# Block-diagonal recurrence products kept as 64-column halves and multiplied as two 64-row products side by side

## What is computed

```python
def step(state, inp):
    r_t, w_t, k_t, v_t, a_t, b_t = inp
    sa = jnp.einsum('bhvk,bhk->bhv', state, a_t)
    state = (state * w_t[:, :, None, :] + sa[..., None] * b_t[:, :, None, :]
             + v_t[..., None] * k_t[:, :, None, :])
    return state, jnp.einsum('bhvk,bhk->bhv', state, r_t)
state0 = jnp.zeros((B, H, N, N), f32)
_, y = lax.scan(step, state0, inputs)
```

## Time and profile before

| | us |
|---|---|
| Three runs: median (lowest to highest) | 1535.57 (1533.57 to 1537.86) |
| The profiled execution's own time | 1534.63 |
| Its span, first to last instruction | 1532.8 |
| TensorE busy | 1434.3 (94%) |
| VectorE, ScalarE, GpSimd busy | 512.3, 324.5, 64.8 |
| The recurrence, first product to start of `branch` | 1188.93 to 1272.26, 83.3 |

### The profile page before, as it was taken

How to read it: one execution, slowest core, us unless ns; L and a number is a source line. 1 busy time by engine, 2 the same in 40 slices (tenths; PEclk the granted TensorE clock), 3 DMA queues, 4 the chain that set the end, 5 groups by cost and what they waited for, 6 DMA issues and landing times.

```text
span 1532.8 us, 21740 instructions
## 1 busy us (share of the span) xinstructions
PE 1434.3 (94%) x9246; PEld 781.6 (51%) x9246; DVE 512.3 (33%) x881; ACT 324.5 (21%) x476; POOL 64.8 (4%) x32
## 2 busy tenths in 40 slices
PE   8989999999999989989989998978999999999998
PEld 6543333333333333333333333328778885499997
DVE  1753111212111111112112111137797446365665
ACT  0531000101100000001001000025655220244442
POOL 0000000000000000000000000000000000023231
PEclk9999999999999999999999999999999999999999
DMA  9699999999999999999999999984452106145552
GB/s 363 259 379 386 428 427 427 428 429 428 428 428 428 429 428 428 428 429 428 428 428 428 428 429 429 428 360 133 151 165 63 49 2 247 41 164 192 179 190 82
DMA packets 44685, 491.44 MB, mean 321 GB/s; under 512 B 4960, under 2 KB 5472, under 8 KB 13184
## 3 DMA queue, kind: packets, MB, share of 16 engines
q1 hardware_dynamic: 44496, 490.66, 77.9%
q10 hardware_dynamic: 144, 0.13, 0.0%
HBM read 489.73 MB, written 1.05 MB: 320 GB/s over the span
## 4 chain that ended last, share of the span: by engine, by line
PE 63%; DMA 28%; DVE 5%; ACT 3%; issue 1%; POOL 0%; SPq 0%; DVEq 0%; ACTq 0%
DMA ring<-in_w_exp 17%; PE bank L778 14%; PE bank L807 9%; DMA work<-in_w_exp 7%; PE bank L836 6%; PE bank L837 6%; PE bank L838 6%; DMA spare<-in_w_exp 3%; PE bank L736 2%; PE bank L724 2%; PE bank L1176 2%; PE bank L673 2%; PE bank L1214 2%; DMA ring<-in_w_lora 1%; PE bank L594 1%; PE bank L624 1%
## 5 line engine op out<-in xcount | busy, mean ns | idle before, releaser
L778 PE MATMUL bank<-ring,spare 128*64 128x512 f32 x1344 | 302.2, 596 | 25.2 <-DMA ring<-in_w_exp 25.2
L1782 DVE TENSOR_SCALAR work<-bank 128x512 f32<-128x512 f32 x32 | 22.1, 692 | 741.2 <-PE bank L778 741.2
L778 PEld LDWEIGHTS bank<-ring,spare 128*64 128x64 f32 x1344 | 92.9, 136 | 221.0 <-issue 160.0
L807 PE MATMUL bank<-ring,spare 128*64 128x512 f32 x672 | 148.8, 595 | 14.7 <-ACT spare L1340 14.7
L778 PE MATMUL bank<-work,spare 128*64 128x512 f32 x576 | 129.7, 595 | 8.2 <-DMA work<-in_w_exp 8.2
L836 PE MATMUL bank<-work_parts,ring_parts 128*128 128x256 f32 x472 | 131.4, 278 | 4.5 <-DVE work_parts L1841 4.5
L1336 ACT ACTIVATE work<-work 128x512 f32<-128x512 f32 x32 | 20.2, 631 | 536.0 <-DVE work L1782 536.0
L837 PE MATMUL bank<-work_parts,ring_parts 128*128 128x256 f32 x472 | 131.9, 280 | 0.0
L838 PE MATMUL bank<-work_parts,ring_parts 128*128 128x256 f32 x472 | 131.8, 279 | 0.0
L807 PEld LDWEIGHTS bank<-ring,spare 128*64 128x64 f32 x672 | 46.9, 137 | 103.2 <-issue 90.4
L836 PEld LDWEIGHTS bank<-work_parts,ring_parts 128*128 128x128 f32 x472 | 89.7, 190 | 5.6 <-issue 4.9
(11 more groups left out here) (395 smaller groups left out, 1688.0 us busy)
## 6 DMA issues: line engine op xcount, KB each, us to landing
ring<-in_w_exp SPq DMA_DIRECT2D x126, 2048.0 KB, 34.6
work<-in_w_exp SPq DMA_DIRECT2D x54, 2048.0 KB, 34.6
spare<-in_w_exp SPq DMA_DIRECT2D x12, 2048.0 KB, 31.4
ring<-in_ffn_up SPq DMA_DIRECT2D x22, 1024.0 KB, 5.3
ring<-in_ffn_down SPq DMA_DIRECT2D x22, 512.0 KB, 3.5
ring<-in_w_in SPq DMA_DIRECT2D x2, 2048.0 KB, 18.5
ring<-in_w_out SPq DMA_DIRECT2D x4, 1024.0 KB, 17.4
ring<-in_w_k SPq DMA_DIRECT2D x4, 1024.0 KB, 5.2
```

The lines of the kernel that those rows point to most:

```text
L778: ins = pe.matmul(to[n2 * CAP:(n2 + 1) * CAP, :], x_e[:, 2 * j + kk, :], w[:, b, kk, n2 * BANK:(n2 + 1) * BANK], start=False, stop=j == UP ...
L807: ins = pe.matmul(y_bank[n2 * CAP:(n2 + 1) * CAP, :], hidT[:, k % 4, k // 4 * CAP:(k // 4 + 1) * CAP], w[:, kk, n2 * BANK:(n2 + 1) * BANK] ...
```

## The change

- The masked matrices keep, for each row of 128 tokens, only the 64 columns of that row's own half. Their tiles (Mb, MA, MoT, NK, P2, PU) shrink from 128 to 64 columns a head, and so do the six masks. "X2" gets a tile of its own.
- Each 128x128 product becomes two 64x64 products, `rows = pair_rows(c2)` for c2 = 0, 1: operands and output lie in partitions 0 to 63 for the one and 64 to 127 for the other, in the same PSUM bank.
- `products` uses two banks instead of four and `key_products` the other two. `key_products` no longer waits for "Mb".
- `products(0, 0)` comes before the wait for pT2_ready; `key_products(0, 0)` and `products(0, 1)` come before the attention product. The second tile row's `products` go into the first one's chunk loop, after chunks 1 and 2 (batch 1 first). All `outputs` come before the chunk loop.
- The wait for x0 moves from "p8" to "x1". VectorE's U2 becomes two instructions a batch instead of four, and its rT two instead of one.

The core of the diff:

```diff
+            PAIRS = range(TT)
+            pair_rows = lambda c2: slice(c2 * HD, (c2 + 1) * HD)
 def products(tt, b):
-                        pe.matmul(B[2 * half][:, i2 * P:(i2 + 1) * P], ar[k, i, 0, cols], b_hat[k, i, cols],
+                            pe.matmul(B[2 + half][rows, i2 * HD:(i2 + 1) * HD], ar[k, i, 0, cols], b_hat[k, i, cols],
 def key_products(tt, b):
-                pe.wait_ge(rec_ready, count(vector_steps, "Mb", tt, b))
...
-            pe.wait_ge(pT2_ready, 1)
             pe.wait_ge(gate_ready, 6)
             products(0, 0)
-
+            pe.wait_ge(pT2_ready, 1)
+            key_products(0, 0)
             pe.wait_ge(pT_ready, 5)
+            products(0, 1)
...
-                        pe.matmul(B[1][:, c], Z["MA"][:, m, 0, :], Z["Mb"][:, m, :], start=m == 0, stop=True, skip_group_check=True)
-                        ins = pe.matmul(B[3][:, c], Z["Mb"][:, m, :], Z["MA"][:, m, 0, :], start=m == 0, stop=True, skip_group_check=True)
+                        for c2 in PAIRS:
+                            rows = pair_rows(c2)
+                            pe.matmul(B[2][rows, m * HD:(m + 1) * HD], Z["MA"][rows, m, 0, :], Z["Mb"][rows, m, :],
+                                      start=m == 0, stop=True, skip_group_check=True)
...
-                        ins = pe.matmul(B[2][:, m * P:(m + 1) * P], Z["MoT"][:, m, :], Z["X1"][:, m, :],
-                                        start=m == 0, stop=True, skip_group_check=True)
+                        for c2 in PAIRS:
+                            rows = pair_rows(c2)
+                            ins = pe.matmul(B[2][rows, m * P:(m + 1) * P], Z["MoT"][rows, m, :], Z["X1"][rows, m, :],
+                                            start=m == 0, stop=True, skip_group_check=True)
...
-                outputs([(0, 1), (0, 3), (1, 0)])
-                between = [[(1, 1)], [(1, 2)], [(1, 3)], []]
+                outputs([(0, 1), (0, 3), (1, 0), (1, 2), (1, 1), (1, 3)])
...
-                    if between[c]:
-                        ins = outputs(between[c])
-                ins.then_inc(y2_done, 1)
+                    if tt == 0 and c in (1, 2):
+                        products(1, 2 - c)
+                    if c == P // CH - 1:
+                        ins.then_inc(y2_done, 1)
```

More of the change, by code:

```diff
@@ L106, in constants2 @@
     row, col = i[:, None], i[None, :]
-    chunk, sub = row // CH == col // CH, row // SUB == col // SUB
+    own, near = row % HD, np.arange(HD)[None, :]
+    chunk, sub = own // CH == near // CH, own // SUB == near // SUB
     t = np.arange(T)
@@ L1065, in _ @@
                     for m in range(4):
-                        ins = pe.matmul(B[1][:, m * P:(m + 1) * P], Z["P2"][:, m, :], Z["PU"][:, m, 1, :],
-                                        start=m == 0, stop=True, skip_group_check=True)
+                        for c2 in PAIRS:
+                            rows = pair_rows(c2)
+                            ins = pe.matmul(B[3][rows, m * HD:(m + 1) * HD], Z["P2"][rows, m, :], Z["PU"][rows, m, 1, :],
+                                            start=m == 0, stop=True, skip_group_check=True)
                     ins.then_inc(rec_done, 1)
@@ L1071, in _ @@
                     pe.wait_ge(rec_ready, count(vector_steps, "U8", tt, b))
+                    pe.wait_ge(rec_copied, count(scalar_steps, "x0", tt, b))
                     for m in range(4):
-                        ins = pe.matmul(B[3][:, m * P:(m + 1) * P], Z["PU"][:, m, 1, :], x0[:, tt, head(b, m)[0], :],
-                                        start=m == 0, stop=True, skip_group_check=True)
+                        for c2 in PAIRS:
+                            rows = pair_rows(c2)
+                            ins = pe.matmul(B[1][rows, m * P:(m + 1) * P], Z["PU"][rows, m, 1, :], x0[rows, tt, head(b, m)[0], :],
+                                            start=m == 0, stop=True, skip_group_check=True)
                     ins.then_inc(rec_done, 1)
@@ L1086, in _ @@
                     for m in range(4):
-                        ins = pe.matmul(B[0][:, m * P:(m + 1) * P], Z["PU"][:, m, 1, :], Z["Mb"][:, m, :],
-                                        start=m == 0, stop=True, skip_group_check=True)
+                        for c2 in PAIRS:
+                            rows = pair_rows(c2)
+                            ins = pe.matmul(B[0][rows, m * P:(m + 1) * P], Z["PU"][rows, m, 1, :], Z["X2"][rows, m, :],
+                                            start=m == 0, stop=True, skip_group_check=True)
                     ins.then_inc(rec_done, 1)
@@ L1096, in _ @@
                             m = 2 * half + i2
-                            ins = pe.matmul(B[1][half * HD:(half + 1) * HD, i2 * P:(i2 + 1) * P], Z["X1"][:, m, 0:HD], Z["MA"][:, m, 1, :],
-                                            start=i2 == 0, stop=True, skip_group_check=True)
+                            for c2 in PAIRS:
+                                rows = pair_rows(c2)
+                                ins = pe.matmul(B[c2][half * HD:(half + 1) * HD, i2 * HD:(i2 + 1) * HD], Z["X1"][rows, m, 0:HD], Z["MA"][rows, m, 1, :],
+                                                start=i2 == 0, stop=True, skip_group_check=True)
                     ins.then_inc(rec_done, 1)
@@ L1500, in _ @@
                     act.wait_ge(rec_done, count(tensor_steps, "x1", tt, b))
-                    act.copy(Z["X1"], four(B[3])).then_inc(rec_copied, 1)
+                    act.copy(Z["X1"], four(B[1])).then_inc(rec_copied, 1)
                 for b in range(2):
```

155 lines of the change are left out of this document (86 added, 69 removed).

## The result

| | before | after |
|---|---|---|
| Timed beside each other: median (lowest to highest) | 1536.24 (1533.57 to 1537.86) | 1512.35 (1511.60 to 1515.04) |
| The profiled execution's own time, its span | 1534.63, 1532.8 | 1512.52, 1510.7 |
| The recurrence, first product to start of `branch` | 83.3 | 59.7 |

The ratio is 0.985, with an interval of 0.983 to 0.987: 23.9 us faster, where 18.5 was forecast. A second comparison gave 0.984 (0.982 to 0.985). The difference is real, inside the range given, and about 5 us larger than the sum.

The account below looks back on a forecast made before the run. TensorE's own work was taken to bound the recurrence; products saved 8.75 us a tile row, 17.5 for both, moves and waits 0.2, partition changes 0.8: gain 18.5, from 1535.57 to 1517.0, range 1511 to 1523.

Parts of the forecast that it names:

- the place and the bound: In the recurrence TensorE's own work sets the pace, 81.6 us busy of 83.4; nothing after it hides the gain.
- the two-part terms: Squares, p4, p8, du, x1 to x3: instructions at 0.031 or 0.055 us save 1.6, 2.45, 1.6, 0.8, 0.1 a tile row.
- products and key_products: they were already two halves abreast … Together nothing: Products go from about 1.3 to 1.38 us, key products from about 0.95 to 0.88 a batch: no gain together.
- rT: TensorE's rT step: 16 at about 0.055 us against 32 at 0.031, 0.1 lost a tile row; waits 0.4 more in all.
- The moves: Reordered steps: products(0, 0) earlier 0.5 us, second-row products covering a wait 0.3, outputs before the loop 0.8, less cover -0.6.
- the last sections: From states to the next squares, or to branch: a gain of 3.8 us over both tile rows.
- Waits: TensorE's waits in the recurrence grow from 2.2 to 3 or 4 us, on VectorE's transitions and x3.
- The first (one bank, no overlap): Halves writing one bank don't run abreast: 32 us more work, kernel 13.5 slower at 1549; chance 4%.
- The second (clock): Half-array products drop the granted clock to 0.50; over the whole recurrence about 1570; chance 3%.
- The third (copies): At du and x1 to x3 copies come late, 14 handovers by 0.4 us: 5.6 lost, gain 13, 1522.5; chance 13%.
- The fourth (64x64 with 128 columns at 0.11): In x1 to x3 and p4 such products cost 0.11 us alone: 14 us lost, gain 4.5, 1531; chance 4%.
- The overhead of about 60 cycles: Skill's warning for small matmuls: 39 instead of 31 ns each, over some 700, gain 13; not subtracted.

Follow-up runs that it names:

- e6a: The changed kernel with every products and key_products step computed twice, four array parts in turn: stretch from last transposes to branch 69.2 us, timed 1517.84, ratio 0.989.
- e6b: The changed kernel with products and key_products computed twice, both passes over one token half first, so blocks use two array parts: stretch 72.3 us, timed 1520.37, ratio 0.991.
- e3: The changed kernel with its half-width products kept but the moved steps put back in the old order: stretch 65.4 us against 62.4, timed 1512.06, ratio 0.985.
- after_again: The changed kernel, unedited, run again: stretch from last transposes to branch 62.6 us against 62.4, timed 1510.62, ratio to before 0.984.
- e1: The changed kernel with diagonal-pair steps issuing all of one half before the other, not in turns: stretch 74.6 us against 62.4, timed 1524.73, ratio 0.993.
- e4: The changed kernel with an extra ScalarE copy ahead of those of P2, P4, P8, X1, X2: stretch 65.0 us, 2.6 longer, timed 1514.33, ratio 0.986.
- e7: The changed kernel with diagonal-pair steps except outputs in blocks of 4 or 8 instructions per half: stretch 65.7 us, 3.3 longer, timed 1516.59, ratio 0.988.
- e5: The changed kernel with states called directly behind each batch's rT: stretch 61.0 us against 62.6 for the unedited rerun, timed 1511.16 against 1510.62.

## Why the prediction was right, and where its size was off

**Right: the place and the bound.** The recurrence was bound by TensorE's work and still is, 56.2 busy of 59.7. Its time fell with the products, and nothing behind it gave the gain back.

**Right: the two-part terms.** Squares 0.93 to 0.98 a batch (forecast 1.0), p4 from 1198.02 to 1199.36, 1.34 a batch (2.75 for two), p8 and du together from 1201.63 to 1204.83, 3.2 (3.0 and a wait of 0.2), x1 to x3 5.4 (5.3). L1157's row and L1005's were the right ones to take them from. Squares to x1 brought 2.1 more than forecast: 0.8 are two key products, below. The rest, about 1.3, are the short gaps between full-width steps: the instruction terms of before add up to 16.8 with a key product, and the section took 17.5, where in after 9.2 of terms took 9.2 to 9.5.

**The step that failed: "products and key_products: they were already two halves abreast … Together nothing".** The forecast priced the new form as two parts taking turns, 16 x 0.031 + 16 x 0.055. In fact half of the rows and half of the columns make four 64x64 parts, and neighbouring instructions of these two steps use all four. The 32 instructions of a product step then take 0.72 us instead of 1.38, and the key products 0.44 to 0.51 instead of 0.88, four times each: 4 x 0.66 + 4 x 0.4 = 4.2 us. rT is the same mistake, smaller. It was put at 0.5 a batch and takes (0.46 - 0.22)/15 x 16 = 0.26, so that the section from rT to `states` gained 0.3 where it was to lose 0.4. Together that is 4.9 of the missing 5.1 us. That the rest is so small is chance: the gaps above brought 1.3 more than forecast, and the last sections, below, 1.3 less. e6a and e6b show the cause: the same instructions at 0.022 us on four parts and at 0.045 on two. The other terms were rightly priced at two parts, since each of their steps uses only the two parts on the diagonal of the array.

**The moves: mis-sized.** Their terms (0.5 + 0.3 + 0.8 - 0.6) add up to 1.0; taking them back costs 2.7 to 3.0 (e3). The prediction measured the moves against waits of before. Yet with half-width outputs the old order would have waited more, 2.6 us at L1191 against 0.9, and the moves' worth is to be read against that. In the sum it shows little: the last sections gained 4.2 where 3.8 was forecast, although their two products and one key product gave 1.7 of it. So some 1.3 us of what was expected in them didn't come. Nearly all of it can be read from the timeline. The wait ahead of the second row's squares is 0.8 instead of 0.5. In the first tile row `states(1)` takes 1.91 us instead of the 1.38 of the second, with an idle time put down to issue in it. There too L1189 starts about 0.2 late, right behind the transitions (L2102), and the 0.3 that the products were to cover is still 0.25. That is 0.3 + 0.5 + 0.2 + 0.25.

**Waits.** 3 to 4 us were forecast in all, 3.1 came. rT has 0.4 twice, as forecast. The squares wait 0.8 instead of 0.5, the wait for the first state behind the transitions is 0.7 (1.0 in after_again) instead of 1.1, and du and x1 to x3 wait for nothing above 0.2.

**The rivals.** The first (one bank, no overlap) is refuted: diagonal pairs write one bank and keep 0.03 us. e1 shows what a loss of part of the overlap costs, 12.2 us. On the Trainium skill's rule in "TensorEngine Tiling (Array Packing)", Gotcha 1, that different row tiles can't access the same PSUM bank at once, the trace of after disagrees for parts with different output partitions, as L1157's row did. The second (clock) didn't occur in any kernel, even with four parts in use. The third (copies) is bounded by e4. The fourth (64x64 with 128 columns at 0.11) is refuted by L1097, L1106 and L1115 at 0.055 to 0.058.

The overhead of about 60 cycles that the same page of the Trainium skill states (Performance Considerations, Instruction Overhead) would have made a small instruction of a pair an estimated 39 ns by the prediction. The trace of after doesn't show it: the squares' spacing is 29 to 31, and that of four parts 22. The prediction doesn't show how 25 ns of overhead become 8 more; half of it for each of two would be an estimated 12.5, and the gain about 10 instead of 13. Neither came.

## What to carry to other kernels

When a product is cut to blocks, read which part of the array each of the next few instructions uses, rows and columns both: blocks on the diagonal give two parts abreast, row halves against column halves give four. One instruction here cost 0.031 or 0.055 us (64 or 128 columns) with two parts, and 0.016 or 0.027 with four (0.022 for the mean of both). Put the parts in turns within about four instructions; longer blocks lost part of the overlap (blocks of 8 cost 0.4 us in a step of 1.0). A moved step is worth what the new, shorter neighbours no longer cover, so price the old order at the new durations before calling a move small.

## What the runs showed of the hardware that was not expected

**Matmuls start out of the program's order.** In after the program alternates four instructions of L981 (two products of two instructions) with four of L985, and the trace shows eight L981 in a row, then eight L985. It is not an order fixed in the program: after and after_again are the same kernel, and of the 1665 starts in their recurrences, counted in order of time, 68 are of another line. In after, for one, the first nv instruction (L1063) starts ahead of the last one of p4 (L1056); in after_again it doesn't. First after, then after_again:

```profile
1199.36 0.22 PE L1063 MATMUL bank<-work,ring 64*64 64x64 f32 x1
1199.38 0.22 PE L1056 MATMUL bank<-ring 64*64 64x64 f32 x1
```

```profile
1199.46 0.32 PE L1056 MATMUL bank<-ring 64*64 64x64 f32 x4
1199.58 0.67 PE L1063 MATMUL bank<-work,ring 64*64 64x64 f32 x16
```

The starts of one step's first instructions also lie among the last of the step before: in e1's records three instructions of L997 start at 1193.99, ahead of the last three of the squares (to 1194.16). All this reads as if an instruction whose part is free passes those whose part is taken, with a reach of about four instructions by e7.

**Four parts at once.** Four parts of the array took the same instructions at 0.022 us that two took at 0.045, at a granted clock of 1.00.

**Idle time behind dense short matmuls.** After the 160 matmuls of the doubled steps in e6a TensorE stood still for 2.63 us ahead of L1014, and no engine released it. The table of busy time by stretch for e6a, columns as in the earlier trace rows, shows 52 instructions in one us and then none:

```profile
1193.00:1194.00 1.00, 1.00 (x52) 0.87 (x46) 0.49 (x2) 0.00 (x0) 0.43 (x1) 1.00 1.03 442
...
1195.00:1196.00 1.00, 0.00 (x0) 0.00 (x0) 1.00 (x5) 0.00 (x0) 0.22 (x1) 1.00 0.00 0
```

The queue that the profile calls instruction moved 9 packets in the recurrence of before and 13 in the shorter one of after (packets, MB, share):

```profile
q8 instruction: 9, 0.15, 0.8%
q8 instruction: 13, 0.21, 1.4%
```

That is one packet for some 250 matmuls and weight loads of TensorE in both (2242 and 3329 in all). In e6a none moved from 1190.2 to 1194, while the other loads kept the DMA engines at 426 to 428 GB/s, and one moved between 1194 and 1195, inside the idle time. That instructions run out when matmuls are this short fits e6a, e6b and e5, where such waits of 0.6 to 2.6 us come behind dense stretches. It is argued from where they stand, not shown. If it is so, it limits what a denser order can bring: e5 has 1.5 us of such idle time and after_again 0.5.
